# Down product of a decoder step: three row groups against seven block products

## The reference, cut to what matters

```
z = rmsnorm(x, g1) @ w_in            # last 2048 columns: the gates, sigmoid(z + b)
m = gate_a * (o_a @ w_proj_a) + gate_b * (o_b @ w_proj_b)
x = x + m @ w_o
u = rmsnorm(x, g2) @ w_up            # 1024 x 5632
c = conv_b + sum_i conv_w[i] * u[row - 2 + i]      # causal, width 3
f = gelu(c[:, :2816]) * c[:, 2816:]
y = rmsnorm(x + f @ w_down, g_f)     # w_down 2816 x 1024; the "down product"
```

## Time and profile before

| | before |
|---|---|
| median of three runs | 1913.81 us |
| the profiled execution's own time | 1909.32 us |
| its span (first to last instruction) | 1906.8 us |
| mean granted TensorE clock | 0.970 of full |
| PE busy | 1782.7 us (93%) |
| PEld (weight loads, overlap PE) | 1522.5 us (80%) |
| DVE busy | 1131.6 us (59%) |
| ACT busy | 794.3 us (42%) |
| POOL busy | 251.0 us (13%) |
| DMA | 331.13 MB, mean 174 GB/s |

### The profile page before, as it was taken

One profiled execution on the slowest core, in us unless ns is written; L12 is line 12 of the kernel. 1 busy time (PEld: TensorE's weight loads), 2 busy tenths in 40 slices (PEclk: granted clock), 3 DMA queues, 4 the chain that ended last, 5 costly groups with the idle time before them and its releaser, 6 DMA issues. The chain is left out here.

```text
span 1906.8 us, 32200 instructions
## 1 busy us (share of the span) xinstructions
PE 1782.7 (93%) x12290; PEld 1522.5 (80%) x12290; DVE 1131.6 (59%) x1935; ACT 794.3 (42%) x1479; POOL 251.0 (13%) x321
## 2 busy tenths in 40 slices
PE   7999999999778887998988999999999999899997
PEld 5777779999445556666668889999999999788875
DVE  5224575443374896666668269677777776445455
ACT  4220013433773585433332144455555554334343
POOL 0000000000100302333200002133223222000000
PEclk9999999999887789999989999999999999999998
DMA  6477742431802927999946335122232222756564
GB/s 233 173 267 266 267 160 73 137 114 48 221 4 67 327 93 273 396 386 386 386 171 213 139 124 175 56 80 68 69 102 69 69 71 86 251 184 204 186 214 137
DMA packets 169826, 331.13 MB, mean 174 GB/s; under 512 B 35769, under 2 KB 97098, under 8 KB 167306
## 3 DMA queue, kind: packets, MB, share of 16 engines
q1 hardware_dynamic: 143242, 193.58, 30.9%
q0 software_dynamic: 26432, 135.50, 19.7%
HBM read 283.02 MB, written 95.68 MB: 199 GB/s over the span
## 5 line engine op out<-in xcount | busy, mean ns | idle before, releaser
L3067 PE MATMUL tl_ps<-tl_dn,tl_f 128*128 128x512 f32 x1144 | 263.5, 392 | 6.5 <-DVE tl_f L2768 4.8
L3067 PEld LDWEIGHTS tl_ps<-tl_dn,tl_f 128*128 128x128 f32 x1144 | 216.4, 190 | 53.2 <-DVE tl_dn L2764 6.5
L3001 PE MATMUL tl_ps<-tl_T_hi,tl_slots 128*128 128x272 f32 x1216 | 211.5, 288 | 1.2 <-ACT tl_u L2453 1.2
L3001 PEld LDWEIGHTS tl_ps<-tl_T_hi,tl_slots 128*128 128x128 f32 x1216 | 175.4, 188 | 1.5 <-ACT tl_u L2453 1.5
L3001 PE MATMUL tl_ps<-tl_X_hi,tl_slots 128*128 128x272 f32 x912 | 161.1, 288 | 0.7 <-ACT tl_u L2522 0.7
L2764 DVE TENSOR_TENSOR tl_dn<-all_lead,tl_dn 128x1024 fp32r<-128x1024 f32 x66 | 80.9, 1225 | 134.9 <-ACT tl_dn L2531 134.9
L763 PE MATMUL fr_ps<-fr_w_hi,h_hi 128*128 128x512 f32 x384 | 152.5, 397 | 2.4 <-DVE h_lo L547 2.4
L763 PE MATMUL fr_ps<-fr_w_lo,h_hi 128*128 128x512 f32 x384 | 151.6, 395 | 0.0
L763 PE MATMUL fr_ps<-fr_w_hi,h_lo 128*128 128x512 f32 x384 | 149.9, 390 | 0.0
L2531 ACT ACTIVATE tl_dn<-all_lead 128x1024 fp32r<-128x1024 f32 x66 | 70.0, 1060 | 159.3 <-PE tl_ps L3067 139.6
L3001 PEld LDWEIGHTS tl_ps<-tl_X_hi,tl_slots 128*128 128x128 f32 x912 | 132.1, 188 | 0.9 <-ACT tl_u L2522 0.9
(11 more groups left out here) (384 smaller groups left out, 3736.4 us busy)
## 6 DMA issues: line engine op xcount, KB each, us to landing
all_lead<-in_w_down SPq DMA_DIRECT2D x66, 512.0 KB, 3.6
out_s<-in_cache POOLq DMA_DIRECT2D x8, 4080.0 KB, 17.8
pg_pages<-in_pool POOLq DMA_DIRECT2D x64, 256.0 KB, 6.3
pg_pages<-in_pool SPq DMA_DIRECT2D x64, 256.0 KB, 7.2
pg_odds<-in_pool SPq DMA_DIRECT2D x64, 256.0 KB, 8.0
all_lead<-in_w_up SPq DMA_DIRECT2D x26, 512.0 KB, 4.7
zs<-fr_zt SPq DMA_DIRECT2D x48, 256.0 KB, 3.7
fd<-tl_c POOLq DMA_DIRECT2D x22, 544.0 KB, 4.9
```

The costliest lines, as they stand in the source:

```text
L3001: last = pe.matmul(ps[:, (bank + n) * 512:(bank + n) * 512 + SIDE // 2], w[:, k, :], h[:, k, n * SIDE // 2:(n + 1) * SIDE // 2], start=(fi ...
L3067: last = pe.matmul(down_bank(m), x, w[:, h * 512:h * 512 + 512], start=(k == 0 and q == 0), stop=(k == FT - 1 and q == len(passes) - 1), s ...
```

## The change

1. **Down product of the prompt rows as seven block products.** f (1024 x 2816) and w_down (2816 x 1024) are cut in quarters (512 x 1408 and 1408 x 512); seven products P1, P6, P2, P5, P3, P7, P4 of 11 steps each, 77 steps, each with four row tiles. A step is one tile of 128 x 1024: 512 columns of f (or a sum of f quarters) and 512 of w_down (or a sum of its quarters). Split steps lie in a ring of 11 places, eight of them over `T_hi`/`T_lo`; raw tiles have four places. Six PSUM banks rotate over the products; P1's banks are also kept in SBUF (`keep`), since they enter several quarters. Sample rows ride on P1 (twice), P2, P5 and P3 with their own two banks and their own operand tiles `fs0`, `fs1`.
2. **Sums of w_down's quarters** (`td`) are made in the gates: 22 parts, each loaded by GpSimd as two DMAs of 256 KB, four VectorE instructions of 128x256, stored as 512 KB; two buffers; four parts per unit.
3. **Sums of f's quarters** (`sd`) are made by GpSimd in the up product: one per column for j < 11, three per column from j = 11 on, with reloads of earlier columns.
4. **The up product's weight sums** go from GpSimd to VectorE.
5. **Residual rows** come back tile by tile, one ahead of each of the steps 5 to 13.
6. The last product runs row tile by row tile, with the last norm behind each; y's first five tiles are stored by GpSimd.

The diff, cut to its core:

```diff
 # front stage, GpSimd
+            def load_part(i):
+                if i >= 2:
+                    pool.wait_ge(wsum_stored[i % 2], 16 * (i // 2))
+                for q in range(2):
+                    pool.dma_start(wsum[:, i % 2, q, :, :], w_parts[i // 2, i % 2, q]).then_inc(wsum_in[i % 2], 16)
+            def store_part(i):
+                pool.wait_ge(wsum_step, 4 * i + 4)
+                pool.dma_start(td[i // 2, :, :, (i % 2) * 256:(i % 2) * 256 + 256], ...).then_inc(wsum_stored[i % 2], 16)
+            load_part(0)
+            load_part(1)
+            for i in range(2 * FH):
+                if 1 <= i < 2 * FH - 1:
+                    load_part(i + 1)
+                store_part(i)
+                if i % 4 == 3 and 3 + i // 4 < NU:
+                    pool.wait_ge(lo_made, 7 * (2 + i // 4))
+                    load_unit(3 + i // 4)
 # front stage, VectorE
+            def sum_part(i):
+                x = wsum[:, i % 2, :, :, :]
+                dve.wait_ge(wsum_in[i % 2], 32 * (i // 2 + 1))
+                dve.tensor_tensor(x[:, 1, 1, :], x[:, 1, 1, :], x[:, 0, 1, :], ALU.subtract).then_inc(wsum_step, 1)
...
                 finish_c22(s_)
+                sum_parts(s_, 0)
...
                     sum_s2(s_ + 1)
+                    sum_parts(s_, 1)
...
                 finish_c12(s_)
+                sum_parts(s_, 2)
...
                     unit_rest(s_ + 1, "S4")
+                sum_parts(s_, 3)
 # tail stage
+        DOWN = ("P1", "P6", "P2", "P5", "P3", "P7", "P4")
+        STEPS = len(DOWN) * FH
+        LEAD = 5
 # SP: load_step(n), then in the loop
+                if n < 4:
+                    sp.wait_ge(lo_made, 7 * (UNITS - 1 + n // 2))
                 else:
-                    sp.wait_ge(dn_lo_done, n - 1)
-                    sp.wait_ge(f_lo_done, n - 1)
+                    sp.wait_ge(step_lo, n - 3)
...
+                if 5 <= n < 5 + RT:
+                    t = n - 5
+                    sp.dma_start(x2[0:rows_of(t), t, :], x2d[t * P:t * P + rows_of(t), :]).then_inc(x2_back, 16)
 # GpSimd
+            def add_sums(j):
+                n, k = sums_made(j - 1), j - FH
+                pool.wait_ge(sums_in, 32 * (k + 1))
+                pool.tensor_tensor(sums[:, 0, :], c[:, 1, HALF2], sums[:, 0, :], ALU.subtract).then_inc(sum_step, 1)
+                pool.tensor_tensor(sums[:, 1, :], c[:, 1, HALF2], sums[:, 1, :], ALU.add).then_inc(sum_step, 1)
+                pool.wait_ge(sum_step, n + 1)
+                pool.tensor_tensor(s4[:, :], c[:, 1, HALF1], sums[:, 0, :], ALU.subtract).then_inc(sum_step, 1)
...
 # ScalarE, last_tap(j, 1)
                         act.wait_ge(f_stored, 16 * j)
+                        act.wait_ge(sum_step, sums_made(j - 1))
...
+            def step_head(n):
+                act.wait_ge(step_in[n % 4], 32 * (n // 4 + 1))
+                step_room(act, n)
+                act.activation(ring[n % FH][:, 0, :], step_raws[n % 4], ACT.Copy).then_inc(step_hi, 1)
 # VectorE
+            def step_rest(n):
+                dve.wait_ge(step_hi, n + 1)
+                dve.tensor_tensor(ring[n % FH][:, 1, :], step_raws[n % 4], ring[n % FH][:, 0, :].bitcast(F32), ALU.subtract).then_inc(step_lo, 1)
...
+                q, after = divmod(n - FH - LEAD, FH)
+                if q >= 0 and after == 0:
+                    for at in range(4):
+                        if DOWN[q] == "P6":
+                            add_kept(at)
+                        else:
+                            for quarter in QUARTERS[DOWN[q]]:
+                                add_out(DOWN[q], at, quarter)
...
+            for at in range(4):
+                add_out("P4", at, (1, 0))
+                finish(1 + at)
 # TensorE
+            def row_tile(n, q, r):
+                k, (hi, lo) = n % FH, (ring[n % FH][:, part, :] for part in range(2))
+                for m, (x, w) in enumerate(three_passes(hi[:, r * P:r * P + P], lo[:, r * P:r * P + P], hi[:, 512:1024], lo[:, 512:1024])):
+                    last = pe.matmul(down_bank(4 * q + r), x, w, start=(k == 0 and m == 0), stop=(k == FH - 1 and m == 2))
...
+            def down(q):
+                for k in range(FH):
+                    pe.wait_ge(step_lo, n + 1)
...
+                    for r in range(4):
+                        if k == 0:
+                            bank_free(4 * q + r)
+                        last = row_tile(n, q, r)
...
+            def last_down():
+                q = len(DOWN) - 1
+                for r in range(4):
+                    bank_free(4 * q + r)
+                    for k in range(FH):
+                        if r == 0:
+                            pe.wait_ge(step_lo, q * FH + k + 1)
+                        row_tile(q * FH + k, q, r)
```

More of the change, by code:

```diff
@@ L55 @@
 UNITS = FT - PLAIN_UP
+FH = FT // 2
 def rows_of(t):
@@ L2226, in bank_pair, with sample_bank, added_before @@
+        def sample_bank(i):
+            return ps[:, S_BANKS[i] * 512:S_BANKS[i] * 512 + 512]
+        def added_before(name, r, quarter):
+            before = [ADDED[what] for what in ADDS[:ADDED[(name, r, quarter)] - 1] if what[1:] == (r, quarter)]
+            return max(before, default=0)
         def bank_pair(b):
@@ new lines, in sample_rests, with add_out @@
+            def sample_rests(i):
+                dve.wait_ge(fs_hi_done, i + 1)
+                dve.tensor_tensor(fs[i][:, :, SROWS:2 * SROWS], fs_raw[:, :, :], fs[i][:, :, 0:SROWS].bitcast(F32),
+                                  ALU.subtract).then_inc(fs_lo_done, 1)
+            def add_out(name, r, quarter):
+                half, side = quarter
+                x = x2[:, 4 * half + r, side * 512:side * 512 + 512]
+                n = 4 * DOWN.index(name) + r
+                if name == "P6":
+                    dve.wait_ge(kept_summed, r + 1)
+                else:
+                    dve.wait_ge(out_ready, n + 1)
+                if name == "P1":
+                    dve.wait_ge(bank_kept, r + 1)
+                before = added_before(name, r, quarter)
+                if before:
+                    dve.wait_ge(added, before)
+                dve.tensor_tensor(x, x, kept[:, r, :] if name == "P6" else down_bank(n), ALU.add).then_inc(added, 1)
@@ L2920, in _ @@
[L2920 to L2931 removed]
+                step_rest(n)
@@ new lines, in _ @@
+                if q == 1 and 1 <= after < 7:
+                    for what in [what for what in ADDS if what[0] == "P6"][2 * after - 2:2 * after]:
+                        add_out(*what)
+                if n == 5 * FH + LEAD + 6:
+                    variance(1, *NORMS[0], RT + FIRST)
+                if n == 5 * FH + LEAD + 8:
+                    roots(0)
+                    for i in range(FIRST):
+                        scale_out(i)
+            for at in range(4):
+                add_out("P4", at, (1, 0))
+                finish(1 + at)
@@ new lines, in bank_free @@
+            def bank_free(n):
+                if n < 4:
+                    pe.wait_ge(*((c21_done, UNITS - 1) if n < 2 else (c11_done, UNITS)))
+                elif n < 6:
+                    pe.wait_ge(c12_done, UNITS)
+                else:
+                    q, r = divmod(n - 6, 4)
+                    if DOWN[q] == "P6":
+                        pe.wait_ge(kept_summed, r + 1)
+                    else:
+                        pe.wait_ge(added, max(ADDED[(DOWN[q], r, quarter)] for quarter in QUARTERS[DOWN[q]]))
@@ new lines, in row_tile, with samples_part @@
+            def row_tile(n, q, r):
+                k, (hi, lo) = n % FH, (ring[n % FH][:, part, :] for part in range(2))
+                for m, (x, w) in enumerate(three_passes(hi[:, r * P:r * P + P], lo[:, r * P:r * P + P], hi[:, 512:1024], lo[:, 512:1024])):
+                    last = pe.matmul(down_bank(4 * q + r), x, w, start=(k == 0 and m == 0), stop=(k == FH - 1 and m == 2))
+                if k == FH - 1:
+                    last.then_inc(out_ready, 1)
+                return last
+            def samples_part(n, half, side, first, final):
+                k, (hi, lo) = n % FH, (ring[n % FH][:, part, 512:1024] for part in range(2))
+                pe.wait_ge(fs_lo_done, half + 1)
+                for m, w in enumerate((hi, lo)):
+                    last = pe.matmul(sample_bank(side), fs[half][:, k, :], w, start=(first and k == 0 and m == 0),
+                                     stop=(final and k == FH - 1 and m == 1))
+                if final and k == FH - 1:
+                    last.then_inc(s_ready, 1)
+                return last
@@ L3113, in _ @@
                     p7(s_ + 1)
-            for n in range(STEPS):
-                down(n)
+            for q in range(len(DOWN) - 1):
+                down(q)
+            last_down()
 def program(nc, a, o, scratch):
```

452 lines of the change are left out of this document (252 added, 200 removed).

## The result

The changed kernel is 0.6% slower: 1925.97 us, the median of 4 runs (1923.49 to 1927.51), against 1913.11 in 4 runs of the kernel before, taken beside them; the ratio is 1.0064, 95% interval 1.005 to 1.0078. That is less than 2%, but clear of the noise. Its profiled span is 1921.8 us against 1906.8, its mean granted clock 0.963 against 0.970.

A forecast was written before the change was run, and what follows sets the result against it. TensorE matmuls, 93% of the span, were taken as the bound. Down product and tail falling from 282.9 to 248.9 us, with 2 us lost in the gates, gave -32.0 us: 1881.8 us, range 1873 to 1903.

The forecast's parts named there:

- The gates' weight sums: Gates: sums of w_down's quarters fit beside the matmuls at a buffer round of 10 us, costing 2 us.
- the prediction's formula: Gates: loss is 5.5 x (2R + 1.9 - 21) - 4 us, R being one buffer's round, taken as 10.
- rival (a): Gates paced by the sums' DMA round, 10.5 to 12.8 us; at 11.5, 15 us lost, 1895 us; chance 0.17.
- (b): Gates: DMA round from 12.8 us on loses 33 us or more; 1915 us at 13.1; chance 0.06.
- Up product: Up product: moving weight sums to VectorE and adding gated-row sums on GpSimd costs 0 us, bounds -1 and +11.
- Its waits: Down product: 1.7 us of small waits at the joins plus 4.0 us in the seventh product.
- The old stall: Down product's start: TensorE idle 4.8 us behind a late w_down load, then partly at 1.2 GHz; taken as gone.
- rival (c): Down product: its stall moves instead of going; 7.5 us stay, plus 2.7 for the clock; 1892 us; chance 0.11.
- Rival (d): Down product: VectorE, blocked in an add, late at six joins, 7.5 us each, 45 in all; 1927 us; chance 0.04.
- The seventh product's stall: Down product's last block product: only six steps ready at its start, so TensorE waits 4.0 us in short waits.
- Tail: After the last matmul: only the last row tile's chain remains, 9.0 us against 16.2, 7.2 us less.
- The sum for the down product and tail: From 1623.9 us to the end: 234.2 + 1.7 + 4.0 + 9.0 = 248.9 us, against 282.9 before.

The follow-up runs named there:

- u1_short_sums: Changed kernel with GpSimd's three sums per gated row, from column 11 on, cut to 8 of 512 columns (output incomplete): 1914.34 us.
- u4_sums_on_dve: Changed kernel with the three sums of a gated row, from column 11 on, made by VectorE; GpSimd only stores them: 1918.44 us.
- c1_best: Changed kernel with three weight-sum buffers, store ahead of load, gated rows' sums on VectorE, samples' second load and gain on GpSimd: 1884.42 us.
- c2_spread: c1_best with residual rows at every second step, and output gain and last rows' store behind step 22: 1878.84 us.
- d1_samples_pool: Changed kernel with the samples' second load and the output gain's load issued by GpSimd instead of SyncE: 1932.14 us.

## Why the prediction was wrong

Forecast 1881.8 us, measured 1926.0. Both of its own signs of being wrong came: gates more than 5 us longer, up stage more than 2. By its steps:

- **The gates' weight sums: the step that failed.** "A buffer's round is sum 1.7, store of 512 KB, load of 512 KB as two DMAs, 0.2 of signals, and two rounds per unit must fit into 21 us" was forecast at +2 us and measured at +34.9. The condition was wrong, more than its terms. It lets the two buffers' rounds overlap, as if only a buffer's own chain counted. But one in-order engine issues both, and the change's order (load i+1, which waits for store i-1, ahead of store i) chains each store behind the landing of the last: a part costs store landing plus load issue, 6.8 us in the mean, not half a round of 10. The prediction's rows for a store with the measured 1.4 us of load issue would have given (2.9 to 4.9) + 1.4 per part, 4.3 to 6.3, with the unit's load 19 to 27 us per unit, so a loss of up to 30 us as an ordinary case. The sizes were at fault only in part: with the measured medians (sum 1.8, store 4.8, second load issued 0.7 later and landing after 3.9, signals 0.2) the round is 11.4 instead of 10, and the prediction's formula then gives 16 us, less than half of 34.9. (That formula also gives 17 us at the R = 11.5 of rival (a), not 15, and 32 at R = 12.8 of (b), not 33; the forecast doesn't rest on either.) Rival (b) named this price (33 us or more) and gave it 0.06, because it was made to hang on two slow rows at once instead of on the order of the queue. Rows, queue and effect on TensorE (idle 21.9 us, the rest half clock) are shown; three buffers with the store first take all but 1.5 us of it away.
- **Up product: 0 forecast, +6.3 measured**, inside its bounds. The mis-sized term is "three GpSimd sums per column may give 1.2 back": they take 3.9 us of VectorE per unit, so that VectorE needs 22.2 us a unit. TensorE keeps its 21.07 until VectorE's lead is used up, and takes 22.2 from 1531 us on. Shown by u1_short_sums and u4_sums_on_dve.
- **Down product's matmuls: right.** 1034, and 1034 x 0.2265 = 234.2 us.
- **Its waits: 5.7 us forecast, 13.1 measured** (247.3 from the first to the last matmul's end, less 234.2). The old stall did go as an event, but 2.1 us at step 3 and 3.8 at the first join with their half clock came in, 9.5 us together: rival (c) in part. Rival (d), VectorE late in an add at a join, is seen at one join of six. Its time, 1927, lies next to the measured 1926 by chance: it put 45 us into the down product, and the loss was in the gates. "Each step moves 1 MB where about 3.7 us of matmuls stand, it fits" overlooked that gated rows' stores, the samples, the gain and the last rows are in the same 45 us. Spread out it did fit. The wait at step 3 goes back, in the chain of waits, to a store of f that took 6.5 us to land (1659.54), behind which ScalarE's and VectorE's last taps stand. But in u1_short_sums the same store takes 6.4 us and the wait is gone; what differs is its start, 9.1 us ahead of the down product instead of 5.5, because VectorE was not held up in front of it. In u4_sums_on_dve, c1_best and c2_spread, which have no such sums on GpSimd either, step 3 has no wait, and step 4 one of 1.2 us, behind VectorE's own three sums. So this term, too, fell with the price of GpSimd's sums. The seventh product's stall was forecast at 4.0 us and is 1.8.
- **Tail: 9.0 forecast, 9.5 measured.** One reading was off: the chain leaves TensorE at 1890.64 because the adds' bank was then complete, while the last matmul of the kernel before starts at 1893.4. So the old tail was 13.0 us, not 16.2, and the old down product had 3.2 us more in waits. The sum from 1623.9 to the end isn't touched by this.
- **The sum for the down product and tail, 248.9 us**, is what c2_spread takes (248.7). That it fits to 0.2 us is luck in part: the wait at step 4 was not in it, the seventh product's stall is 1.7 us in place of 4.0, the tail half a us longer. But the forecast was near for a kernel in which neither a queue nor GpSimd's sums got in the way.

Open: why the middle's time differs by up to 12 us between kernels that do the same there; no run here isolates it. Which share of the first join's wait each of the transfers in that crowd has is open too.

## What to carry to other kernels

Where one engine issues both the stores and the loads of a ring of buffers, write out its queue as a loop and time one turn of it: a wait in front of an instruction is a wait for all that follow, and the number of buffers only counts if the order lets it (two buffers: 6.8 us a part in one order, 8.3 in the other; three: 5.1, under the 5.3 that the unit leaves). Before work goes to GpSimd to relieve VectorE, count GpSimd's whole duration as time that VectorE may lose, not as nothing. And a load that "fits by mean bandwidth" is to be placed with everything else that runs in those microseconds.

## What the hardware showed that was not expected

- The same load of the samples' columns (two issues, 352 KB in 128-byte pieces) held SyncE for 1.58 us at 1659.38 and for 6.72 us at 1684.53, when the DMA engines were full (392 GB/s over those 6.8 us); issued by GpSimd in such a crowd (370 GB/s, in d1_samples_pool) it took 2.19.
- GpSimd's 128x512 sums take 1.28 to 1.30 us in the up product's units from column 11 on, though VectorE wants to run; VectorE's rest takes its own length plus all three. In the last column, where they take turns with rests of 1.2 us, each takes 2.3. In the kernel before both had been seen slowed, too (1.50 and 1.74 us).
- At each of the gates' six waits (2.0 to 5.4 us) and the two early ones of the down product (2.1 and 3.8) the granted clock fell to half for a while: some of the gates' matmuls took 306 ns in the mean in place of 287. In the gates that is what is left of the 34.9 us beside 21.9 idle, 13 us. Behind the wait of 1.3 us at 1888.91 it did not fall (1.00 over 1885 to 1910).
